# Expert products of the further jobs: plain float32 operands in place of split pairs, and the next rows turned ahead of the down product

## Chip, core and metric

One core of a Trainium2 chip runs the kernel in one launch. The metric is the device time of that launch in microseconds (us), the median of several runs.

## What is computed

One block of a decoder: a convolution branch and an attention branch are merged by gates and added to the input, and a mixture of experts follows. Only the experts matter here. Each of the 2048 tokens picks 2 of 64 experts; its normalized row of 1024 numbers goes through each of the two.

```
def expert_block(args):
    xb, e = args
    hb = jax.nn.silu(xb @ w_gate[e]) * (xb @ w_up[e])
    return hb @ w_down[e]
```

w_gate[e] and w_up[e] are 1024 x 256, w_down[e] is 256 x 1024, all float32. The two results of a token are weighted and added to its row afterwards.

## The kernel before

The kernel runs six stages one after another: project, attend, merge, route, experts, combine. The route stage writes a table that lists for each expert the rows that chose it. The experts stage works in **jobs** of up to 128 rows of one expert. Jobs 0 to 63 are the first tiles of the 64 experts ("first jobs"). Where an expert has more than 128 rows, a further tile follows: the "further jobs", number 64 and up. Their count and their experts are known only at run time, so each engine reads the count from job_sb and runs them in a loop with conditions (over_further_jobs).

One job takes these steps. The buffers are double, and b is the job's parity:
- SyncE (SP) loads gate and up weights (weights_gate_up, 2 x 1 MB, L1903) and down weights (weights_down, 1 MB, L1907) with load_gate_up and load_down.
- VectorE (DVE) writes the list of row numbers (index, L2278). POOL gathers the rows by it from memory into rows (gather, L2090, an indirect DMA).
- TensorE (PE) turns the rows in 8 transposes into x_bank (turn_rows, L2145).
- ScalarE (ACT) takes xT_hi from x_bank (high_x, L2216), DVE the rest xT_lo (lower_x, L2289). Both are float32r. In the same way gate and up weights are split in two halves of 2048 columns each: ACT makes gu_hi (high_gate_up, L2210), DVE makes gu_lo (lower_gate_up, L2284).
- PE makes gate and up products in gu_bank (gate_up, by pair_matmuls, L91 to L93): for each of 8 chunks hi x hi, hi x lo and lo x hi, 24 products of 512 columns.
- ACT applies silu (gate, L2222), DVE multiplies by up (times_up, L2295), PE turns the result (turn_hidden, L2165, two transposes), ACT takes it as hT (take_hidden, L2227).
- PE makes the down product on plain float32 operands (down, L2175). A plain float32 product appears in the trace as two records, so the 4 products of a job are 8 records.
- ACT takes y out of PSUM (take_y, L2233). POOL scatters it to memory (scatter, L2098, an indirect DMA).

The order of the work on each engine is written out by hand. For the further jobs it is the list `parts` given to over_further_jobs: in each turn the parts run in that order, those marked True for job n+1 (ahead), those marked False for job n. For job 63, the last first job, the same parts run once in front of the loop, with n = 63 and 64. In one turn the engines do this, in order:
- PE: gate_up(n), turn_hidden(n), turn_rows(n+1), down(n)
- ACT: high_gate_up(n+1), gate(n), take_hidden(n), high_x(n+1), take_y(n)
- DVE: index(n+1), lower_gate_up(n+1), times_up(n), lower_x(n+1), take_list(n)
- POOL: gather(n+1), scattered(n-1), scatter(n)
- SP: load_gate_up(n+1), which waits until the buffer's former weights are split (gu_lo_ready), and load_down(n+1), which waits for the down product of job n-1 (down_done)

Of the kernel before, what the change touches and what calls it, by code (L numbers as in the profile page):

```python
# [30 lines left out]
P = 128  # L31
# [52 lines left out]
def raw(ap):  # L84

    return ap.bitcast(F32)
# [1824 lines left out]
def stage_experts(nc, weights, hn_d, table_d, jobs_d, y_d):  # L1911
# [10 lines left out]
    with ExitStack() as ctx:  # L1922
# [13 lines left out]
        rows = sb("rows", [P, 2, D])  # L1936
        xT_hi = sb("xT_hi", [P, 2, DC, P], F32R)
        xT_lo = sb("xT_lo", [P, 2, DC, P], F32R)
        silu = sb("silu", [P, DE])
        hidden = sb("hidden", [P, 2, DE])  # L1940
        hT = sb("hT", [P, 2, HC, P])
# [84 lines left out]
        @block.sync  # L2026
        def _(sp):
            sp.dma_start(table[:, :], table_rows[0:P, :]).then_inc(table_loaded, 16)
            sp.dma_start(job_sb[:, 0:1 + 2 * MORE_JOBS], jobs_d).then_inc(jobs_loaded, 16)

            def load_gate_up(n, b, e):
                wait(sp, gu_lo_ready, n * 2 + 2)
                weights.load_gate_up(sp, b, e)

            def load_down(n, b, e):
                wait(sp, down_done, n + 1)
                weights.load_down(sp, b, e)

            load_gate_up(2, 0, 2)
            load_gate_up(3, 1, 3)  # L2040
            wait(sp, jobs_loaded, 16)
            count = sp.value_load(job_sb[0:1, 0:1], min_val=0, max_val=MORE_JOBS)

            def load_list(j):
                e = sp.value_load(job_sb[0:1, bass.ds(j + 1, 1)], min_val=0, max_val=EXPERTS - 1)
                first = sp.value_load(job_sb[0:1, bass.ds(j + (1 + MORE_JOBS), 1)], min_val=0, max_val=SEQ - P)
                sp.dma_start(columns[:, bass.ds(j, 1)], table_rows[bass.ds(first, P), bass.ds(e, 1)],
                             allow_slow_non_contiguous=True).then_inc(columns_loaded, 16)

            with sp.Fori(0, MORE_JOBS // LISTS) as i:  # L2050
                with sp.If(i * LISTS < count):
                    for k in range(LISTS):
                        with sp.If(i * LISTS + k < count):
                            load_list(i * LISTS + k)

                    sp.sem_inc(pair_passed["SP"], 1)
            load_down(2, 0, 2)
            with sp.Fori(2, EXPERTS // 2) as q:
                for b in range(2):
                    n = q * 2 + b  # L2060
                    load_gate_up(n, b, n)
                    load_down(n - 1, 1 - b, n - 1)
            load_down(EXPERTS - 1, 1, EXPERTS - 1)

            def further(n, b, q):
                j = n - EXPERTS + 1
                e = sp.value_load(job_sb[0:1, j:j + 1] if isinstance(j, int) else job_sb[0:1, bass.ds(j, 1)],
                                  min_val=0, max_val=EXPERTS - 1)
                load_gate_up(n, b, e)
                load_down(n, b, e)  # L2070

            over_further_jobs(sp, [(True, further)])

# [59 lines left out]
        def _(pe):  # L2133
# [15 lines left out]
            def gate_up(n, b, half):  # L2149
# [7 lines left out]
                if half:  # L2157
                    m.then_inc(gu_done, 1)

            def turn_hidden(n, b):  # L2160

                pe.wait_ge(hidden_ready, n + 2)
                by_chunk = hidden[:, b, :].rearrange("t (p c) -> t c p", c=HC)
                for c in range(HC):
                    m = nc.tensor.transpose(gu_bank[:, b, c * P:(c + 1) * P], by_chunk[:, c, :], ident[:, :])  # L2165
                m.then_inc(hidden_turned, 1)
# [25 lines left out]
            down(EXPERTS - 2, 0, EXPERTS // 2 - 1)  # L2192

            def further_products(n, b, q):
                gate_up(n, b, 0)
                gate_up(n, b, 1)
                turn_hidden(n, b)

            over_further_jobs(pe, [(False, further_products), (True, turn_rows), (False, down)])

        @block.scalar
        def _(act):
# [53 lines left out]
            take_hidden(EXPERTS - 2, 0)  # L2256
            take_y(EXPERTS - 2, 0)

            def further_weights(n, b, q):
                for half in range(2):  # L2260
                    high_gate_up(n, b, q, half)

            def further_hidden(n, b, q):
                gate(n, b)
                take_hidden(n, b)

            over_further_jobs(act, [(True, further_weights), (False, further_hidden),
                                    (True, lambda n, b, q: high_x(n, b)), (False, lambda n, b, q: take_y(n, b))])

        @block.vector  # L2270
        def _(dve):
# [15 lines left out]
            def lower_x(n, b):  # L2287
                wait(dve, x_hi_ready, n + 1)
                nc.vector.tensor_tensor(xT_lo[:, b, :, :], x_bank[:, :, :].rearrange("p k (c t) -> p (k c) t", t=P),  # L2289
                                        raw(xT_hi[:, b, :, :]), ALU.subtract).then_inc(x_lo_ready, 1)  # L2290

            def times_up(n, b):
                wait(dve, silu_ready, n + 1)
# [35 lines left out]
                j = n - EXPERTS  # L2329
                return columns[:, j:j + 1] if isinstance(j, int) else columns[:, bass.ds(j, 1)]  # L2330

            def further_weights(n, b, q):
                index(n, b, further_list(n))
                for half in range(2):
                    lower_gate_up(n, b, half)

            def further_rows(n, b, q):
                take_list(n, b, list_of(n) if isinstance(n, int) and n < EXPERTS else further_list(n))

            over_further_jobs(dve, [(True, further_weights), (False, lambda n, b, q: times_up(n, b)),  # L2340
                                    (True, lambda n, b, q: lower_x(n, b)), (False, further_rows)])


def stage_combine(nc, h_d, y_d, weight_d, out):
# [130 lines left out]
```

## Time and profile before

| | |
|---|---|
| median of 3 runs | 3007.86 us (3005.77 to 3012.45) |
| profiled execution, its own time | 3009.71 us |
| its span | 3007.8 us |
| mean granted TensorE clock | 0.933 |
| busy share: PE, DVE, ACT, POOL | 85%, 58%, 38%, 17% |
| mean memory traffic | 170 GB/s |

The profile is of one execution. The busy share of an engine is a mean over six stages that have different limits, so it tells what an engine does in total, and not what bounds a stage; for that one reads windows and timelines of the stage itself.

### The profile page before, as it was taken

To read this page: it belongs to the slowest core of one execution; us is meant where nothing else is said; L and a number is where in the kernel's file an instruction comes from. 1 tells how busy PE (TensorE), PEld (TensorE's weight loads), DVE (VectorE), ACT (ScalarE), POOL (GpSimd) and SP (SyncE) were. 2 spreads that over 40 slices of the span, in tenths; PEclk is the share of its full clock that TensorE was granted. 3 is DMA by queue.
4 is the path that set the end of the run, shared out by engine and by line. 5 is a ranking of instruction groups with operands and counts; after the bars stand their busy time and mean duration, and the time that the engine had idled before them with its cause. 6 is when DMAs were issued, how large, how long until landed. Compare 5 with 4: busy or idle time off the path is not lost. (4 is left out here: it accounts for less than half of the span.)

```text
span 3007.8 us, 40627 instructions
## 1 busy us (share of the span) xinstructions
PE 2543.5 (85%) x12335; PEld 2047.1 (68%) x12335; DVE 1730.5 (58%) x2408; ACT 1145.1 (38%) x1622; POOL 509.1 (17%) x465
## 2 busy tenths in 40 slices
PE   4999999999997598899939886997499999999750
PEld 3888889899985487788817665775366666666530
DVE  6576584967712487787845453444455555555425
ACT  4110111134412376677732222212355555656420
POOL 2122222211100011111103221011211111211110
PEclk9999999999998799999969997998699999999975
DMA  5121211213321533434058867554388889988739
GB/s 127 51 84 37 81 49 63 70 71 106 106 95 59 143 86 87 112 100 132 15 141 193 194 171 228 175 174 181 110 334 331 338 341 368 349 335 344 281 133 394
DMA packets 227934, 510.61 MB, mean 170 GB/s; under 512 B 30268, under 2 KB 150076, under 8 KB 189404
## 3 DMA queue, kind: packets, MB, share of 16 engines
q1 hardware_dynamic: 194738, 411.80, 41.5%
q10 hardware_dynamic: 10626, 55.14, 4.5%
q0 software_dynamic: 22448, 42.16, 4.2%
q8 instruction: 63, 1.03, 0.1%
q14 instruction: 59, 0.48, 0.1%
HBM read 413.28 MB, written 133.46 MB: 182 GB/s over the span
## 5 line engine op out<-in xcount | busy, mean ns | idle before, releaser
L91 PE MATMUL project_bank<-project_xnT_hi,project_w_hi 128*128 128x512 f32 (+4 forms) x1352 | 512.1, 379 | 0.8 <-DVE project_xnT_lo L593 0.7
L92 PE MATMUL project_bank<-project_xnT_lo,project_w_hi 128*128 128x512 f32 (+4 forms) x1352 | 499.9, 370 | 0.0
L93 PE MATMUL project_bank<-project_xnT_hi,project_w_lo 128*128 128x512 f32 (+4 forms) x1352 | 497.8, 368 | 0.0
L2284 DVE TENSOR_TENSOR experts_gu_lo<-weights_gate_up,experts_gu_hi 128x2048 fp32r<-128x2048 f32 x136 | 306.4, 2289 | 134.3 <-ACT experts_gu_hi L2210 133.8
L641 DVE SCALAR_TENSOR_TENSOR project_work<-project_work,project_taps 128x2048 f32<-128x2048 f32 x128 | 341.4, 2667 | 18.6 <-DVE project_work L637 0.6
L2210 ACT ACTIVATE experts_gu_hi<-weights_gate_up 128x2048 fp32r<-128x2048 f32 x136 | 259.2, 1911 | 96.5 <-DMA weights_gate_up<-in_w_up_dram 70.6
L91 PEld LDWEIGHTS project_bank<-project_xnT_hi,project_w_hi 128*128 128x128 f32 (+1 forms) x1352 | 252.5, 187 | 35.6 <-issue 6.7
L92 PEld LDWEIGHTS project_bank<-project_xnT_lo,project_w_hi 128*128 128x128 f32 (+1 forms) x1352 | 252.4, 187 | 32.9 <-issue 6.1
L93 PEld LDWEIGHTS project_bank<-project_xnT_hi,project_w_lo 128*128 128x128 f32 (+1 forms) x1352 | 252.6, 187 | 26.9
L1013 DVE TENSOR_TENSOR attend_pT<-attend_t_bank,attend_pT 128x512 fp32r<-128x512 f32 (+3 forms) x352 | 212.5, 615 | 86.2 <-ACT attend_pT L963 83.8
L2175 PE MATMUL experts_y_bank<-weights_down,experts_hT 128*128 128x512 f32 x544 | 248.8, 600 | 3.9 <-issue 3.3
L909 PE MATMUL attend_o_bank<-attend_pT,attend_values 128*128 128x256 f32 x1216 | 226.9, 303 | 13.1 <-DVE attend_pT L1013 12.4
L963 ACT ACTIVATE attend_pT<-attend_t_bank 128x512 fp32r<-128x512 f32 (+3 forms) x352 | 183.8, 540 | 137.0 <-PE attend_t_bank L895 111.0
L91 PE MATMUL experts_gu_bank<-experts_gu_hi,experts_xT_hi 128*128 128x512 f32 x544 | 228.1, 419 | 0.0
L93 PE MATMUL experts_gu_bank<-experts_gu_hi,experts_xT_lo 128*128 128x512 f32 x544 | 215.6, 396 | 0.0
L92 PE MATMUL experts_gu_bank<-experts_gu_lo,experts_xT_hi 128*128 128x512 f32 x544 | 213.5, 392 | 0.0
L2289 DVE TENSOR_TENSOR experts_xT_lo<-experts_x_bank,experts_xT_hi 128x1024 fp32r<-128x1024 f32 x68 | 83.3, 1225 | 208.3 <-ACT experts_xT_hi L2216 186.1
L475 ACT ACTIVATE project_work<-project_bank,project_bias 128x512 f32<-128x512 f32 x64 | 44.2, 690 | 402.2 <-PE project_bank L93 402.2
L882 PE MATMUL attend_s_bank<-attend_keys,attend_q_hi 128*128 128x400 f32 (+5 forms) x352 | 136.0, 386 | 71.1 <-DMA attend_decay<-decay_d 42.5
L895 PE MATMUL attend_t_bank<-attend_ident,attend_probs 128*128 128x128 f32 x1216 | 192.4, 277 | 0.0
L909 PEld LDWEIGHTS attend_o_bank<-attend_pT,attend_values 128*128 128x128 f32 x1216 | 169.1, 190 | 29.0 <-issue 14.3
L2175 PEld LDWEIGHTS experts_y_bank<-weights_down,experts_hT 128*128 128x128 f32 x544 | 103.5, 193 | 111.0 <-issue 105.8
(249 smaller groups left out, 4316.8 us busy)
## 6 DMA issues: line engine op xcount, KB each, us to landing
weights_gate_up<-in_w_gate_dram SPq DMA_DIRECT2D x68, 1024.0 KB
weights_gate_up<-in_w_up_dram SPq DMA_DIRECT2D x68, 1024.0 KB
weights_down<-in_w_down_dram SPq DMA_DIRECT2D x68, 1024.0 KB, 6.6
project_w_raw<-in_w_in_dram SPq DMA_DIRECT2D x36, 512.0 KB, 4.1
qk_d<-project_work SPq DMA_DIRECT2D x16, 1032.0 KB, 5.3
gate_d<-project_work ACTq DMA_DIRECT2D x16, 1024.0 KB, 3.9
merge_gates<-gate_d SPq DMA_DIRECT2D x64, 256.0 KB, 5.3
merged_d<-merge_m_pair SPq DMA_DIRECT2D x64, 256.0 KB, 4.1
```

Source lines behind the costliest of these rows:

```text
L91: pe.matmul(out, lhs[0], rhs[0], start=first, stop=False)
L92: pe.matmul(out, lhs[0], rhs[1], start=False, stop=False)
L93: return pe.matmul(out, lhs[1], rhs[0], start=False, stop=last)
L641: nc.vector.scalar_tensor_tensor(out=work[:, 2, 0:SEQ], in0=work[:, 1, META - 1 + q:META - 1 + q + SEQ], scalar=taps[:, bass.ds(ct, 1), q] ...
L882: nc.tensor.matmul(out, q_hi[:, h, qs], keys[:, h, a - PAD:e - PAD], start=True, stop=False)
L895: m = nc.tensor.transpose(t_bank[:, j % 3, (t % 4) * P:(t % 4 + 1) * P], probs[:, u % BUF, t * P:(t + 1) * P], ident[:, :])
L909: m = nc.tensor.matmul(out, values[:, h, t, :], pT[:, j % 3, t % 4].rearrange("p k q -> p (k q)"), start=t == 0, stop=t == last)
L963: nc.scalar.activation(pT[:, j % 3, 0:n, 0, :], t_bank[:, j % 3, 0:n * P].rearrange("p (t q) -> p t q", q=P), ACT.Copy)\
L1013: nc.vector.tensor_tensor(pT[:, j % 3, 0:n, 1, :], t_bank[:, j % 3, 0:n * P].rearrange("p (t q) -> p t q", q=P), raw(pT[:, j % 3, 0:n, 0, ...
L2175: m = nc.tensor.matmul(y_bank[:, b, half, :], hT[:, b, c, :], down_raw[:, b, c, cols], start=c == 0, stop=c == HC - 1)
L2210: nc.scalar.activation(gu_hi[:, b, :, cut, :], gu_raw[:, b, :, cut, :], ACT.Copy)\
L2284: nc.vector.tensor_tensor(gu_lo[:, b, :, cut, :], gu_raw[:, b, :, cut, :], raw(gu_hi[:, b, :, cut, :]), ALU.subtract).then_inc(gu_lo_ready, 1)
```

## The change

For further jobs from 64 on, the loop jobs, gate and up products use plain float32 operands: xT, a copy of the turned rows, and the loaded weights themselves. The split of rows and weights is gone for them, and with it 24 products of float32r pairs; 8 plain products take their place. Job 63, which runs in front of the loop, keeps the split. The order of the parts changes on PE, ACT and DVE. The load of gate and up weights for a further job now waits for gu_done, the products that read the buffer before, since no split frees it any more.

```diff
+        xT = sb("xT", [P, 2, DC, P])
...
+            def load_further(n, b, e):
+                wait(sp, gu_done, n + 1)
+                weights.load_gate_up(sp, b, e)
+                load_down(n, b, e)
...
-                load_gate_up(n, b, e)
-                load_down(n, b, e)
+                load_further(n, b, e)
...
+            def gate_up_plain(n, b, q):
+                pe.wait_ge(gu_loaded[b], q * 32 + 32)
+                pe.wait_ge(x_lo_ready, n + 2)
+                for c in range(DC):
+                    m = nc.tensor.matmul(gu_bank[:, b, :], xT[:, b, c, :], gu_raw[:, b, :, c, :],
+                                         start=c == 0, stop=c == DC - 1)
+                m.then_inc(gu_done, 1)
...
             def further_products(n, b, q):
-                gate_up(n, b, 0)
-                gate_up(n, b, 1)
+                if isinstance(n, int):
+                    gate_up(n, b, 0)
+                    gate_up(n, b, 1)
+                else:
+                    gate_up_plain(n, b, q)
+
+            def further_down(n, b, q):
                 turn_hidden(n, b)
-
-            over_further_jobs(pe, [(False, further_products), (True, turn_rows), (False, down)])
+                down(n, b, q)
+
+            over_further_jobs(pe, [(False, further_products), (True, turn_rows), (False, further_down)])
...
-            def further_weights(n, b, q):
-                for half in range(2):
-                    high_gate_up(n, b, q, half)
-
-            def further_hidden(n, b, q):
+            def further_products(n, b, q):
                 gate(n, b)
                 take_hidden(n, b)
-
-            over_further_jobs(act, [(True, further_weights), (False, further_hidden),
-                                    (True, lambda n, b, q: high_x(n, b)), (False, lambda n, b, q: take_y(n, b))])
+                take_y(n, b)
+
+            over_further_jobs(act, [(False, further_products)])
...
+            def take_x(n, b):
+                wait(dve, x_turned, n + 3)
+                wait(dve, gu_done, n + 1)
+                nc.vector.tensor_copy(xT[:, b, :, :], x_bank[:, :, :].rearrange("p k (c t) -> p (k c) t", t=P))\
+                  .then_inc(x_lo_ready, 1)
...
-            def further_weights(n, b, q):
+            def further_index(n, b, q):
                 index(n, b, further_list(n))
-                for half in range(2):
-                    lower_gate_up(n, b, half)
...
-            over_further_jobs(dve, [(True, further_weights), (False, lambda n, b, q: times_up(n, b)),
-                                    (True, lambda n, b, q: lower_x(n, b)), (False, further_rows)])
+            over_further_jobs(dve, [(True, further_index), (True, lambda n, b, q: take_x(n, b)),
+                                    (False, lambda n, b, q: times_up(n, b)), (False, further_rows)])
```

PE, the end of a turn of the loop before: the last products of job n, then turn_hidden (L2165), turn_rows of job n+1 (L2145) and down (L2175).

```order
L93 MATMUL experts_gu_bank<-experts_gu_hi,experts_xT_lo 128x512
L2165 MATMUL experts_gu_bank<-experts_ident_e,experts_hidden 128x128 x2
L2019 UNCONDITIONAL_BRANCH
L2016 REGISTER_ALU
L2016 COMPARE_AND_BRANCH
L2141 ISA
L2142 REGISTER_ALU
L2145 MATMUL experts_x_bank<-experts_ident_e,experts_rows 128x128 x8
L2016 UNCONDITIONAL_BRANCH
L2019 COMPARE_AND_BRANCH
```

What the change makes of it: PE, the turn in the changed loop, where L2169 is gate_up_plain, L2150 turn_rows, L2178 turn_hidden and L2188 down:

```order
L2169 MATMUL experts_gu_bank<-weights_gate_up,experts_xT 128x512 x8
L2020 UNCONDITIONAL_BRANCH
L2017 REGISTER_ALU
L2017 COMPARE_AND_BRANCH
L2146 ISA
L2147 REGISTER_ALU
L2150 MATMUL experts_x_bank<-experts_ident_e,experts_rows 128x128 x8
L2017 UNCONDITIONAL_BRANCH
L2020 COMPARE_AND_BRANCH
L2175 REGISTER_ALU
L2178 MATMUL experts_gu_bank<-experts_ident_e,experts_hidden 128x128 x2
L2182 ISA
```

Before, turn_hidden stands between the products and turn_rows. In the change it has moved from ahead of turn_rows to behind it, directly in front of down.

DVE, the same turn before, from the split of the second half of job n+1's weights (L2284) over times_up (L2295) to lower_x (L2289):

```order
L2284 TENSOR_TENSOR experts_gu_lo<-weights_gate_up,experts_gu_hi 128x2x1024 [waits experts_gu_hi_ready]
L2016 UNCONDITIONAL_BRANCH
L2019 COMPARE_AND_BRANCH
L74 REGISTER_ALU
L2295 TENSOR_TENSOR experts_hidden<-experts_silu,experts_gu_bank 128x256 [waits experts_silu_ready,experts_hidden_turned]
L2019 UNCONDITIONAL_BRANCH
L2016 COMPARE_AND_BRANCH
L74 REGISTER_ALU
L2289 TENSOR_TENSOR experts_xT_lo<-experts_x_bank,experts_xT_hi 128x1024 [waits experts_x_hi_ready]
```

DVE, the turn in the changed loop, where L2310 is take_x and L2316 times_up:

```order
L2293 TENSOR_SCALAR experts_from_row<-experts_columns 128x1
L2017 UNCONDITIONAL_BRANCH
L2017 COMPARE_AND_BRANCH
L74 REGISTER_ALU
L74 REGISTER_ALU [waits experts_x_turned]
L2310 COPY experts_xT<-experts_x_bank 128x1024 [waits experts_gu_done]
L2017 UNCONDITIONAL_BRANCH
L2020 COMPARE_AND_BRANCH
L74 REGISTER_ALU
L2316 TENSOR_TENSOR experts_hidden<-experts_silu,experts_gu_bank 128x256 [waits experts_silu_ready,experts_hidden_turned]
```

The work on the turned rows of job n+1 stood behind times_up of job n and now stands ahead of it.

## Rows read from the trace of the kernel before

**Rows 1.** The page's busy times, and its group of the down products.

```profile
PE 2543.5 (85%) x12335; PEld 2047.1 (68%) x12335; DVE 1730.5 (58%) x2408; ACT 1145.1 (38%) x1622; POOL 509.1 (17%) x465
...
L2175 PE MATMUL experts_y_bank<-weights_down,experts_hT 128*128 128x512 f32 x544 | 248.8, 600 | 3.9 <-issue 3.3
```

**Rows 2.** Timeline of PE: start us, us, instruction, [idle before <- releaser].

```profile
2763.72 3.60 PE L2175 MATMUL experts_y_bank<-weights_down,experts_hT 128*128 128x512 f32 x8
2767.16 1.05 PE L2145 MATMUL experts_x_bank<-experts_ident_e,experts_rows 128*128 128x128 f32 x8
...
2840.39 1.97 PE L2145 MATMUL experts_x_bank<-experts_ident_e,experts_rows 128*128 128x128 f32 x8 [2.21 <-DMA experts_rows<-hn_d,experts_from_row]
...
2859.99 1.97 PE L2145 MATMUL experts_x_bank<-experts_ident_e,experts_rows 128*128 128x128 f32 x8 [5.02 <-DMA experts_rows<-hn_d,experts_from_row]
2861.76 4.80 PE L2175 MATMUL experts_y_bank<-weights_down,experts_hT 128*128 128x512 f32 x8
...
2874.68 0.70 PE L2165 MATMUL experts_gu_bank<-experts_ident_e,experts_hidden 128*128 128x128 f32 x2 [2.65 <-DVE experts_hidden L2295]
2880.19 1.97 PE L2145 MATMUL experts_x_bank<-experts_ident_e,experts_rows 128*128 128x128 f32 x8 [4.81 <-DMA experts_rows<-hn_d,experts_from_row]
...
2895.88 1.97 PE L2145 MATMUL experts_x_bank<-experts_ident_e,experts_rows 128*128 128x128 f32 x8
2897.64 3.93 PE L2175 MATMUL experts_y_bank<-weights_down,experts_hT 128*128 128x512 f32 x8
2901.01 0.79 PE L91 MATMUL experts_gu_bank<-experts_gu_hi,experts_xT_hi 128*128 128x512 f32 x1
...
2906.66 0.39 PE L93 MATMUL experts_gu_bank<-experts_gu_hi,experts_xT_lo 128*128 128x512 f32 x1
2908.44 0.51 PE L2165 MATMUL experts_gu_bank<-experts_ident_e,experts_hidden 128*128 128x128 f32 x2 [1.38 <-DVE experts_hidden L2295]
2909.58 3.70 PE L2175 MATMUL experts_y_bank<-weights_down,experts_hT 128*128 128x512 f32 x8 [0.64 <-ACT experts_hT L2227]
```

**Rows 3.** Windows: length, busy us of PE, PEld, DVE, ACT, POOL; PEclk, DMA share, GB/s.

```profile
2600.00:2800.00 200.00, 194.76 (x800) 134.84 (x799) 117.51 (x114) 120.16 (x115) 38.51 (x38) 1.00 0.88 337
...
2860.00:2865.00 5.00, 5.00 (x13) 3.14 (x14) 1.38 (x3) 1.02 (x1) 0.00 (x0) 0.58 0.02 5
...
2870.00:2875.00 5.00, 2.35 (x11) 1.64 (x10) 4.62 (x3) 1.84 (x2) 2.98 (x1) 0.94 1.00 348
```

**Rows 4.** Timeline of POOL: gathers (L2090) and scatters (L2098).

```profile
2798.87 1.02 POOL L2090 DMA_INDIRECT experts_rows<-hn_d,experts_from_row  x1 [7.72 <-DVE experts_to_row L2300]
...
2831.48 1.05 POOL L2090 DMA_INDIRECT experts_rows<-hn_d,experts_from_row  x1 [3.69 <-issue]
...
2868.73 0.99 POOL L2098 DMA_INDIRECT y_d<-experts_y_sb,experts_to_row  x1 [15.94 <-ACT experts_y_sb L2233]
2870.03 2.98 POOL L2090 DMA_INDIRECT experts_rows<-hn_d,experts_from_row  x1 [0.31 <-issue]
...
2890.55 2.95 POOL L2090 DMA_INDIRECT experts_rows<-hn_d,experts_from_row  x1 [0.48 <-issue]
2903.75 0.99 POOL L2098 DMA_INDIRECT y_d<-experts_y_sb,experts_to_row  x1 [10.25 <-ACT experts_y_sb L2233]
```

**Rows 5.** Timeline of ACT.

```profile
2866.82 1.03 ACT L2233 ACTIVATE experts_y_sb<-experts_y_bank 128x1024 f32<-128x1024 f32 x1 [3.57 <-PE experts_y_bank L2175]
```

**Rows 6.** Timeline of SP's queue: the issues of gate weights for jobs 65 and 67.

```profile
2827.02 0.34 SPq L1903 DMA_DIRECT2D weights_gate_up<-in_w_gate_dram  x1
...
2868.83 0.34 SPq L1903 DMA_DIRECT2D weights_gate_up<-in_w_gate_dram  x1
```

**Rows 7.** Timeline of DVE.

```profile
2863.39 1.23 DVE L2289 TENSOR_TENSOR experts_xT_lo<-experts_x_bank,experts_xT_hi 128x1024 fp32r<-128x1024 f32 x1 [8.98 <-ACT experts_xT_hi L2216]
...
2869.80 4.49 DVE L2284 TENSOR_TENSOR experts_gu_lo<-weights_gate_up,experts_gu_hi 128x2048 fp32r<-128x2048 f32 x2 [5.02 <-ACT experts_gu_hi L2210]
...
2894.71 0.41 DVE L2295 TENSOR_TENSOR experts_hidden<-experts_silu,experts_gu_bank 128x256 f32<-128x256 f32 x1
```

## Prediction

> **What bounds the kernel now.** I began with the page's busy table and slices, to see how much of the kernel the change can reach. TensorE is busy 85% of the span [rows 1], but the change leaves the 64 first jobs alone but for what follows job 63's product; only the further jobs see it. Their number is read from the matmul groups: L2175 has 544 records, eight per job (3.60 us for eight [rows 2]), so 68 jobs, 4 of them further: 64 to 67. I call R64 to R67 the starts of their row transposes on TensorE (L2145): 2840.39, 2859.99, 2880.19 and 2895.88 [rows 2]. Everything to be won or lost lies between 2827.02, where the load for job 65 is issued [rows 6], and the start of the combine stage.
>
> Next the windows. Among the first jobs TensorE is busy 194.76 of 200 us at a granted clock of 1.00; behind R65 the clock is 0.58, in part the low level of 1.2 GHz [rows 3]. So the further jobs are not bound by TensorE. The timeline names the bound: the transposes of jobs 64, 65 and 66 wait for DMA experts_rows [rows 2]. I then followed that gather back on POOL. The rows of job 66 are gathered at 2870.03, right behind the scatter of job 64 at 2868.73 [rows 4], which waits for y of job 64 at 2866.82 [rows 5], which waits for the down product at 2861.76 [rows 2], which TensorE issues behind the transposes of job 65. So the circle is: transposes, down product of the job before, y, scatter, gather, next transposes. It takes 19.60, 20.20 and 15.69 us, 55.5 in all. Gate and up products (6.04 us, 2901.01 to 2907.05) and the splitting lie in its shadow, except in job 67, which nothing follows.
>
> Two parts of the circle are longer than they must be. First, the gathers of jobs 65 to 67 keep POOL busy for 2.9 to 3.0 us each, that of job 64 for 1.05, the first jobs' for 1.02 [rows 4]. The long ones begin inside a splitting operation of VectorE: for job 66 its two halves run 4.49 us from 2869.80 [rows 7]. The gather ends 0.97 us after the first half (2869.80 + 2.24 = 2872.04, to 2873.01), as if it had started only there. I read that as POOL being held out by the subtraction of two SBUF tensors. Second, from the end of POOL's work to the transposes pass 7.9, 7.2 and 7.2 us, but only 2.4 for job 67, the one gather that has no gate and up load beside it: the one for job 67 is issued at 2868.83 [rows 6], and the DMA engines move 348 GB/s at share 1.00 in 2870 to 2875 [rows 3].
>
> **The change, part by part.**
> Job 64 starts: SyncE now waits for job 63's product (about 2830.4 instead of 2827.02) before it loads job 65's gate and up [rows 6]. POOL still issues job 64's gather at 2831.48, so gather and load overlap as before, yet the load (2 MB at 348 GB/s: 6 us) is over near 2838, where the rows have come in only near 2840 till now. R64 between 2836.4 and 2840.4; I take -1.5.
> Splitting: for four jobs ACT's copies and DVE's subtractions of the weights go (4 x 4.49 = 18 us of busy time on DVE), worth nothing by themselves, since they lay behind the waiting gather; with them goes the hold on POOL: 1.9 us per gather, three times. For job 64's gather there is no such gain.
> New order: the down product stood 1.77 us behind R. Now VectorE first copies the turned rows (take_x), and only behind that, in its own queue, does times_up follow; then turn_hidden, hT, down. No row shows this copy; the nearest is the subtraction from the same bank, 1.23 us, and on the other side ACT's copy of as many elements from PSUM, 1.03 [rows 5, 7]; I take 1.2, since it is the same engine. times_up is 0.41 [rows 7], and turn_hidden to down 1.14 us at the high clock (2908.44 to 2909.58), 0.2 more at the low one. With transposes of 1.05 to 1.16 or 1.97 us [rows 2] the down product starts at R+4.0 (2.4 GHz) or R+5.1 (1.2 GHz): 2.2 to 3.3 us later than now. That is the change's cost in the circle.
> From down to gather: 8.27 us now (2861.76 to 2870.03), 7.4 if it runs at the high clock (2897.64 to the scatter at 2903.75, plus the 1.3 from scatter to gather) [rows 2, 4]. For the first turn, behind a long idle time, I take 8.7.
> Landing: the loads of 66 and 67 now wait for the products of 64 and 65, which end near R65 and R66, so they are through well before the next gather and still some 8 us ahead of their own use. Landing 2.4 us; for job 65, whose tile may hold more rows, 3.0. Ends: 2.4 and 7.2.
> Product: 16 plain records at the pace of L2175 (3.60 us for eight) make 7.2 us against 6.04. In the circle TensorE then needs 4.0 + 3.4 (down, 2897.64 to 2901.01) + 7.2 = 14.6 us at the high clock, just inside the gather's path, so this stays hidden but takes all the slack there was.
> Sum. R64 to R65, behind 8 us of idle TensorE, clock low: 5.1 + 8.7 + 1.05 + 3.0 = 17.8 against 19.60: -1.8. R65 to R66: 4.0 + 7.4 + 1.05 + 2.4 = 14.9 at the high clock, 5.1 + 8.4 + 1.05 + 2.4 = 17.0 at the low; TensorE's idle time ahead of R now is below 1 us, so I take 15.5, nearer the high: -4.7. R66 to R67 the same 15.5 against 15.69: -0.2. Tail, to the end of job 67's product: now 11.2 us (2895.88 to 2907.05), then 14.6 to 16.6, I take 15.2: +4.0. What follows (silu, down, scatter, barrier, combine) is as before. In all -1.5 - 1.8 - 4.7 - 0.2 + 4.0 = **-4.2 us**.
> The sum is made against the profiled execution: span 3007.8, time 3009.71, so 1.9 us around it. The median of the runs, 3007.86, is 1.9 lower; taken off there, 3003.7 us. A measurement of this kernel tells 0.2%, 6.0 us, from no change; the three runs before span 6.7.
>
> Beside the hold on POOL stands the Trainium skill, SBUF — State Buffer, "Who interferes with whom": a VectorE instruction with two SBUF inputs contends with a GpSimd instruction that reads SBUF, and whoever started first holds the port for the whole instruction. Job 66's gather agrees. But the same section infers that building descriptors needs the write side only, so that tensor_tensor would not stall such a DMA; by that the 2.9 us are something else and stay (rival B), and the sum would be +1.3. That the gather ends one gather's time behind the subtraction's half speaks against it.
>
> **The rivals.**
> A, more is won, 18%: the clock stays high in all four turns and job 64's rows land by 2836.4. Then -4.0, -2.6, -5.3, -0.8 and +3.4: -9.3, 2998.6 us. For it: a gap of 1.38 us left turn_hidden at its fast 0.51 (2908.44). Against: one of 2.65 us did not (0.70 at 2874.68) [rows 2].
> B, the gathers stay at 2.95 us, 12%: because their waits are counted in registers, say. Against: the first jobs' gathers in the loop do that too and take 1.02. +1.9, +1.8, +1.8: 3009.2.
> C, landing stays at 7.2 us for jobs 65 and 66, 10%: the scatter ahead of the gather, not the loads, is what it waits for. +4.2 and +4.8: 3012.7. Against: job 67's has a scatter ahead of it too.
> D, slower, 15%: the clock. The new order cuts TensorE's work at R into transposes, a gap of 1.7 us, two transposes, a gap of 0.6, the down product; today transposes and down are one piece, and the clock rises inside down (4.80 us at 2861.76 instead of 3.60). If it stays at 1.2 GHz through down, eight records at twice 0.43 us make 6.8, 3.2 more than now at the high clock. Each turn is then 5.1 + (7.4 + 3.2) + 1.05 + 2.4 = 19.2, the first 19.8, the tail 5.1 + 6.6 + 7.2 = 18.9: +0.2, -1.0, +3.5, +7.7, with R64 +8.9; if it rises only inside the products, some 1.5 us more each, +15. Middle +12: 3019.9. The turning point is where the clock rises: it costs more than the forecast gains once down takes above some 5.4 us in all four turns. For it: the 0.58 behind R65 [rows 3]. Against: gate and up now run right up to the transposes.
> The Trainium skill, TensorE: Matmul & The Clock Gate, "HAM oscillation", warns of this: work cut up by waits falls back to half rate and must warm up again each time. The windows agree for today's turns; whether gaps this short do it no row tells.
>
> **How the numbers follow.** The forecast has 45%, its own range 3000 to 3007. Predicted 3003.7. Leaving out a fourth of A and most of D gives 2998 to 3014. Faster by over 6.0 us: most of A and a tenth: 0.25. Slower by over 6.0: D and a little of C: 0.17. Within: 0.58.
>
> **What would show it.** Gathers of 65 to 67 at 1.0 us on POOL. R64 near 2839; R to R about 17.8, 15.5, 15.5. down at R+4 to 5. Gate and up products of 7.2 us, 16 records. Loads of 66 and 67 issued at the products' ends; DMA idle when the gather goes. The prediction is wrong if a transpose waits over 4 us for its rows behind a 1 us gather (C), if down takes over 5.4 us (D), or if the next product waits for its weights.

## The result, and the profile after

The change made the kernel slower by a little: the ratio to the kernel before is 1.0023, 95% interval 1.0015 to 1.0031 (medians 3013.55 and 3004.97 us). Two of the 20 runs of the change took 3142 and 9305 us, in a slow state of the chip, and are left out of the ratio. I had forecast 4.2 us less, and called slower by over 0.2% the least likely outcome. Single executions of either kernel differ by some 10 us, so traces are compared here over one stretch that holds all that the change touches: from the start of job 62's down product to the first load of the combine stage. Before it runs from 2821.22 to 2921.05, 99.8 us; after from 2819.97 to 2925.53, 105.6 us: +5.7.

Timeline of PE after, the stretch without job 63's split products and some rows of the later turns (start us, us, instruction, [idle before <- releaser]). L2150 are the row transposes, L2178 turn_hidden, L2188 down, L2169 the plain products.

```profile
2819.97 3.67 PE L2188 MATMUL experts_y_bank<-weights_down,experts_hT 128*128 128x512 f32 x8 [1.21 <-issue]
...
2839.70 1.97 PE L2150 MATMUL experts_x_bank<-experts_ident_e,experts_rows 128*128 128x128 f32 x8 [10.61 <-DMA experts_rows<-hn_d,experts_from_row]
2843.32 0.70 PE L2178 MATMUL experts_gu_bank<-experts_ident_e,experts_hidden 128*128 128x128 f32 x2 [1.65 <-DVE experts_hidden L2316]
2844.54 5.37 PE L2188 MATMUL experts_y_bank<-weights_down,experts_hT 128*128 128x512 f32 x8 [0.52 <-issue]
2849.74 7.03 PE L2169 MATMUL experts_gu_bank<-weights_gate_up,experts_xT 128*128 128x512 f32 x16
2858.51 1.15 PE L2150 MATMUL experts_x_bank<-experts_ident_e,experts_rows 128*128 128x128 f32 x8 [1.74 <-DMA experts_rows<-hn_d,experts_from_row]
2861.62 0.70 PE L2178 MATMUL experts_gu_bank<-experts_ident_e,experts_hidden 128*128 128x128 f32 x2 [1.95 <-DVE experts_hidden L2316]
2862.96 6.41 PE L2188 MATMUL experts_y_bank<-weights_down,experts_hT 128*128 128x512 f32 x8 [0.64 <-ACT experts_hT L2246]
...
2877.05 1.15 PE L2150 MATMUL experts_x_bank<-experts_ident_e,experts_rows 128*128 128x128 f32 x8 [0.82 <-DMA experts_rows<-hn_d,experts_from_row]
...
2881.59 5.40 PE L2188 MATMUL experts_y_bank<-weights_down,experts_hT 128*128 128x512 f32 x8 [0.94 <-ACT experts_hT L2246]
...
2894.65 1.15 PE L2150 MATMUL experts_x_bank<-experts_ident_e,experts_rows 128*128 128x128 f32 x8 [0.80 <-DMA experts_rows<-hn_d,experts_from_row]
...
2898.89 5.40 PE L2188 MATMUL experts_y_bank<-weights_down,experts_hT 128*128 128x512 f32 x8 [0.64 <-ACT experts_hT L2246]
2904.12 7.03 PE L2169 MATMUL experts_gu_bank<-weights_gate_up,experts_xT 128*128 128x512 f32 x16
```

Against [rows 2]: from job 65 on the transposes wait only 0.8 to 1.7 us for their rows, where those of jobs 65 and 66 waited 5.0 and 4.8. In return a gap of 1.65 to 1.95 us stands behind the transposes, released by times_up (DVE L2316), where before down followed at once (before, the wait for times_up stood ahead of the transposes, 2.65 us in the turn of R66 [rows 2]), and down begins 4.2 to 4.8 us behind them instead of 1.8. And down itself takes 5.37 to 6.41 us, where it took 4.80 in the turn of R65 and 3.93 in that of R67.

Windows of the same kernel (length, busy us of PE, PEld, DVE, ACT, POOL; PEclk, DMA share, GB/s):

```profile
2844.00:2849.00 5.00, 4.48 (x8) 2.01 (x8) 0.00 (x0) 0.38 (x1) 0.00 (x0) 0.60 0.00 0
...
2863.00:2868.00 5.00, 5.00 (x6) 2.14 (x7) 0.00 (x0) 0.00 (x0) 0.00 (x0) 0.50 0.14 57
```

TensorE is fully busy in the second window and runs at 0.50, the level of 1.2 GHz, throughout. Timelines of POOL, of DVE and of ACT after:

```profile
2853.30 1.03 POOL L2095 DMA_INDIRECT experts_rows<-hn_d,experts_from_row  x1 [0.45 <-issue]
...
2872.77 1.04 POOL L2095 DMA_INDIRECT experts_rows<-hn_d,experts_from_row  x1 [0.31 <-issue]
...
2890.58 1.03 POOL L2095 DMA_INDIRECT experts_rows<-hn_d,experts_from_row  x1 [0.49 <-issue]
```

```profile
2860.01 1.23 DVE L2310 COPY experts_xT<-experts_x_bank 128x1024 f32<-128x1024 f32 x1 [16.62 <-PE experts_x_bank L2150]
2861.15 0.41 DVE L2316 TENSOR_TENSOR experts_hidden<-experts_silu,experts_gu_bank 128x256 f32<-128x256 f32 x1
```

```profile
2857.05 0.38 ACT L2241 ACTIVATE experts_silu<-experts_gu_bank 128x256 f32<-128x256 f32 x1 [6.08 <-PE experts_gu_bank L2169]
```

The gathers took 1.03 to 1.04 us instead of 2.9 to 3.0 [rows 4], and the copy, which no row before showed, 1.23. Term by term, in us:

| term | forecast | measured | from |
|---|---|---|---|
| down of job 62 to R64 | -1.5 | +0.6 | 19.17 to 19.73 |
| R64 to R65 | -1.8 | -0.8 | 19.60 to 18.81 |
| R65 to R66 | -4.7 | -1.7 | 20.20 to 18.54 |
| R66 to R67 | -0.2 | +1.9 | 15.69 to 17.60 |
| R67 to the product's end | +4.0 | +5.3 | 11.17 to 16.50 |
| to the combine stage | 0 | +0.4 | 14.00 to 14.38 |
| sum | -4.2 | +5.7 | |

### The profile page after: what moved, and what is told of

It reads as the page before. It is cut to its first block and busy times, and to the rows that moved or that the text cites. A ratio compares the mean times of both kernels' runs of the same rounds, so it can differ in the third digit from the quotient of the medians.

```text
span 3012.3 us, 40485 instructions
## 1 busy us (share of the span) xinstructions
PE 2546.0 (85%) x12303; PEld 2038.0 (68%) x12303; DVE 1712.2 (57%) x2400; ACT 1126.3 (37%) x1610; POOL 503.4 (17%) x465
## 3 DMA queue, kind: packets, MB, share of 16 engines
q8 instruction: 63, 1.03, 0.1%
## 5 line engine op out<-in xcount | busy, mean ns | idle before, releaser
L2299 DVE TENSOR_TENSOR experts_gu_lo<-weights_gate_up,experts_gu_hi 128x2048 fp32r<-128x2048 f32 x128 | 288.3, 2289 | 99.8 <-ACT experts_gu_hi L2229 99.5
L2229 ACT ACTIVATE experts_gu_hi<-weights_gate_up 128x2048 fp32r<-128x2048 f32 x128 | 244.5, 1912 | 80.4 <-DMA weights_gate_up<-in_w_up_dram 55.2
L2188 PE MATMUL experts_y_bank<-weights_down,experts_hT 128*128 128x512 f32 x544 | 253.2, 609 | 7.6 <-issue 4.4
L91 PE MATMUL experts_gu_bank<-experts_gu_hi,experts_xT_hi 128*128 128x512 f32 x512 | 214.1, 418 | 0.0
L93 PE MATMUL experts_gu_bank<-experts_gu_hi,experts_xT_lo 128*128 128x512 f32 x512 | 203.0, 397 | 0.0
L92 PE MATMUL experts_gu_bank<-experts_gu_lo,experts_xT_hi 128*128 128x512 f32 x512 | 200.8, 392 | 0.0
L2188 PEld LDWEIGHTS experts_y_bank<-weights_down,experts_hT 128*128 128x128 f32 x544 | 104.8, 194 | 118.4 <-issue 110.1
```

Of the source, the lines that this page charges most:

```text
L91: pe.matmul(out, lhs[0], rhs[0], start=first, stop=False)
L92: pe.matmul(out, lhs[0], rhs[1], start=False, stop=False)
L93: return pe.matmul(out, lhs[1], rhs[0], start=False, stop=last)
L2188: m = nc.tensor.matmul(y_bank[:, b, half, :], hT[:, b, c, :], down_raw[:, b, c, cols], start=c == 0, stop=c == HC - 1)
L2229: nc.scalar.activation(gu_hi[:, b, :, cut, :], gu_raw[:, b, :, cut, :], ACT.Copy)\
L2299: nc.vector.tensor_tensor(gu_lo[:, b, :, cut, :], gu_raw[:, b, :, cut, :], raw(gu_hi[:, b, :, cut, :]), ALU.subtract).then_inc(gu_lo_ready, 1)
```

## The experiments

Ratios are to the kernel before, run beside each on the same chip. "Stretch" is the one above: 99.8 us before, 105.6 after. "Landing" is the time from the end of POOL's gather to the transposes.

**1. The old order with plain operands.** Theory 1 says that the order costs, its rival that the plain products do.

```diff
             def further_products(n, b, q):
...
                     gate_up_plain(n, b, q)
-            def further_down(n, b, q):
                 turn_hidden(n, b)
-                down(n, b, q)
-            over_further_jobs(pe, [(False, further_products), (True, turn_rows), (False, further_down)])
+            over_further_jobs(pe, [(False, further_products), (True, turn_rows), (False, down)])
...
-            over_further_jobs(dve, [(True, further_index), (True, lambda n, b, q: take_x(n, b)),
-                                    (False, lambda n, b, q: times_up(n, b)), (False, further_rows)])
+            over_further_jobs(dve, [(True, further_index), (False, lambda n, b, q: times_up(n, b)),
+                                    (True, lambda n, b, q: take_x(n, b)), (False, further_rows)])
```

> Plain operands and the late load as in the change, but the order of the kernel before on PE (product, turn_hidden, turn_rows, down) and DVE (times_up ahead of take_x). Theory 1, the new order is what costs: down again stands 1.8 us behind R, the gather's path is 1.8 + 8.4 + 1.0 + 3.1 = 14.3 us, and TensorE itself becomes the bound: down to R+6.2, product 7.0, 2.8 to turn_hidden, 0.5: turns of 16.4 us (now 18.8, 18.5, 17.6), the product of job 67 ends at R67+12.2 (now 16.5). Against the kernel before: -5 to -6 us, 0.998. Rival, the plain product is what costs: turns stay at 17.6 to 18.8 and the time at 1.002.

Measured: 0.9953 (0.9937 to 0.9969), stretch 89.7 us. Timeline of PE:

```profile
2849.70 0.50 PE L2178 MATMUL experts_gu_bank<-experts_ident_e,experts_hidden 128*128 128x128 f32 x2 [1.40 <-DVE experts_hidden L2313]
2850.13 1.15 PE L2150 MATMUL experts_x_bank<-experts_ident_e,experts_rows 128*128 128x128 f32 x8
2851.12 3.60 PE L2188 MATMUL experts_y_bank<-weights_down,experts_hT 128*128 128x512 f32 x8
2854.55 7.03 PE L2169 MATMUL experts_gu_bank<-weights_gate_up,experts_xT 128*128 128x512 f32 x16
2862.96 0.51 PE L2178 MATMUL experts_gu_bank<-experts_ident_e,experts_hidden 128*128 128x128 f32 x2 [1.38 <-DVE experts_hidden L2313]
2863.38 1.15 PE L2150 MATMUL experts_x_bank<-experts_ident_e,experts_rows 128*128 128x128 f32 x8
```

The sign was as theory 1 had it, and the size larger than the 5 to 6 us that I expected: 14 us by the ratio, 10 by the stretch, with turns of 15.8, 13.3 and 13.5 us, not 16.4. From job 65 on the circle through the gather is gone, the transposes wait for nothing, and one gap of 1.4 us a turn is all that TensorE idles. There the clock stays at 1.00 and down takes 3.60 to 3.70 us. In the turn of R64, behind 9.2 us in which TensorE waits for the rows, down takes 5.32 us in this order too. The plain operands, with the later load that comes with them, are the gain, and the new order more than spends it.

**2. One line of it.** PE keeps the new order; only VectorE's order is the old one (the second hunk above alone).

> The change, with one thing undone: on DVE times_up stands ahead of take_x again. PE keeps the new order. Theory 1 (the wait of times_up behind take_x is the cost, by itself and by the gap it makes for TensorE's clock): turn_hidden follows the transposes at once, down starts at R+2.3 to 3.3 instead of 4.2 to 4.8 and runs at the high clock (3.7 to 4.5 us, now 5.4 to 6.4); turns 14.5 to 16, job 67's product ends at R67+13, 8 to 9 us below the kernel before, 0.997. Rival, TensorE's order by itself costs: down stays at 5.4 us and the time within 2 us of the change.

Measured: 0.9962 (0.9948 to 0.9976), stretch 91.1 us.

```profile
2859.23 1.15 PE L2150 MATMUL experts_x_bank<-experts_ident_e,experts_rows 128*128 128x128 f32 x8 [0.71 <-DMA experts_rows<-hn_d,experts_from_row]
2860.22 0.40 PE L2178 MATMUL experts_gu_bank<-experts_ident_e,experts_hidden 128*128 128x128 f32 x2
2861.57 3.70 PE L2188 MATMUL experts_y_bank<-weights_down,experts_hT 128*128 128x512 f32 x8 [0.94 <-ACT experts_hT L2246]
```

turn_hidden now follows the transposes without a gap, since times_up was done before them. So nearly the whole loss hangs on take_x standing ahead of times_up on VectorE. The 14.5 us between the two stretches (105.6 and 91.1) come almost wholly from two sources: over the four turns down starts 8.8 us sooner (at R+2.9, 2.0, 2.3 and 2.0 instead of 4.8, 4.5, 4.5 and 4.2), and it runs 5.6 us shorter (5.90, 3.70, 3.70, 3.70 instead of 5.37, 6.41, 5.40, 5.40).

**3. The gaps filled.** Is that second part the clock?

```diff
+            def fill(b, count):
+                for c in range(count):
+                    nc.tensor.matmul(gu_bank[:, b, 0:P], ident[:, :], ident[:, :], start=True, stop=True)
+
+            def further_turn(n, b, q):
+                turn_rows(n, b, q)
+                fill(b, 12)
...
                 turn_hidden(n, b)
+                fill(1 - b, 4)
                 down(n, b, q)
...
-            over_further_jobs(pe, [(False, further_products), (True, turn_rows), (False, further_down)])
+            over_further_jobs(pe, [(False, further_products), (True, further_turn), (False, further_down)])
```

> The change, with TensorE's gaps filled: 12 products of the identity (128 columns) behind the transposes and 4 behind turn_hidden, written to the bank that the next product overwrites. They compute nothing that is used. Theory 2, the clock: down falls from 5.4 to 6.4 us to 3.7 in the turns of jobs 65 to 67, turns become 16.5 and 16, the product of job 67 ends at R67+14.8: 5 to 6 us below the change, about 1.000 of the kernel before. If the low clock in down has another cause (the transposes, the weight loads), down stays at 5.4, and the fill only delays turn_hidden: at or above the change, 1.002 to 1.003.

Measured: 1.0001 (0.9987 to 1.0015), stretch 101.1 us, 4.5 below the change.

```profile
2854.99 1.15 PE L2150 MATMUL experts_x_bank<-experts_ident_e,experts_rows 128*128 128x128 f32 x8 [1.75 <-DMA experts_rows<-hn_d,experts_from_row]
2855.99 2.84 PE L2216 MATMUL experts_gu_bank<-experts_ident_e 128*128 128x128 f32 x24
2858.66 0.40 PE L2178 MATMUL experts_gu_bank<-experts_ident_e,experts_hidden 128*128 128x128 f32 x2
2858.90 1.06 PE L2216 MATMUL experts_gu_bank<-experts_ident_e 128*128 128x128 f32 x8
2859.79 3.61 PE L2188 MATMUL experts_y_bank<-weights_down,experts_hT 128*128 128x512 f32 x8
```

```profile
2860.00:2865.00 5.00, 5.00 (x13) 2.13 (x12) 0.00 (x0) 1.02 (x1) 0.00 (x0) 1.00 0.26 64
```

Nothing but useless products was added, and down fell to 3.60 to 3.70 us in all four turns, at a clock of 1.00. Over the four turns down is 8.1 us shorter than in the change, which is what the clock was worth; the fill itself delays its start by 3.8 us, and the stretch is 4.5 us shorter. Turns of 19.5, 16.3 and 16.3 us.

**4. The order alone, on split operands.** The kernel before, with turn_rows ahead of turn_hidden, and high_x and lower_x ahead of take_hidden and times_up. The edit on VectorE, one of three:

```diff
-            over_further_jobs(dve, [(True, further_weights), (False, lambda n, b, q: times_up(n, b)),
-                                    (True, lambda n, b, q: lower_x(n, b)), (False, further_rows)])
+            over_further_jobs(dve, [(True, further_weights), (True, lambda n, b, q: lower_x(n, b)),
+                                    (False, lambda n, b, q: times_up(n, b)), (False, further_rows)])
```

> The kernel before with the new order alone: products stay split, loads wait for the split as before; turn_rows stands ahead of turn_hidden, and high_x and lower_x ahead of times_up and take_hidden. Theory 1: without the gain of the plain operands (the hold on POOL, 1.9 us, and the landing beside a load, 4 us) the order costs its full 3.5 us per turn: turns of 23 us, the product of job 67 ends at R67+15.5, together some 12 to 14 us above the kernel before, 1.004. Rival, the order costs little: turns near 20 us and a time within 0.1% of the kernel before.

Measured: 1.009 (1.0075 to 1.0105), stretch 125.2 us, 25.4 above the kernel before: about twice the 12 to 14 that I had expected.

```profile
2886.70 1.97 PE L2145 MATMUL experts_x_bank<-experts_ident_e,experts_rows 128*128 128x128 f32 x8 [7.74 <-DMA experts_rows<-hn_d,experts_from_row]
2891.71 0.70 PE L2165 MATMUL experts_gu_bank<-experts_ident_e,experts_hidden 128*128 128x128 f32 x2 [3.04 <-DVE experts_hidden L2298]
2893.11 5.42 PE L2175 MATMUL experts_y_bank<-weights_down,experts_hT 128*128 128x512 f32 x8 [0.70 <-ACT experts_hT L2230]
```

Two steps, ACT's high_x and VectorE's lower_x, stand in the gap here; it is 3.04 us, and down starts at R+6.4 and takes 5.42 us (6.57 in the turn of R65). Turns of 25.6, 26.2 and 20.7 us.

**5. The late load alone.** The kernel before, with `wait(sp, gu_done, n + 1)` in place of the wait for the split.

> The kernel before with one piece of the change: the gate and up load of a further job waits for the products (gu_done) and no longer for the split. Order and split stay. Theory 3, landing beside a load costs: job 66's load moves from 2848.2 only to 2852, job 67's from 2868.8 to 2872, both still beside the gather, since the split holds the gather back to 2852.8 and 2873.0. So the gain is small: landing 5 to 7 us, turns 18 to 20 us, 0 to 4 us below the kernel before, 0.999 to 1.000, and the gathers stay at 2.9 us. Rival, the late load by itself is the gain of the plain operands: turns of 16 us, 0.996.

Measured: 1.0004 (0.999 to 1.0018). Timelines of POOL and of SP's queue:

```profile
2852.04 2.88 POOL L2091 DMA_INDIRECT experts_rows<-hn_d,experts_from_row  x1 [0.45 <-issue]
```

```profile
2854.38 0.34 SPq L1903 DMA_DIRECT2D weights_gate_up<-in_w_gate_dram  x1
```

As expected, the split still holds the gather until 2854.92, beside the later load; landing stayed at 7.5 us. By itself this piece gains nothing: 1 lies within the interval, and the stretch is 103.1 us, 3.3 above the kernel before. R64 comes 19.73 us behind job 62's down, 0.56 later than before and just as in the change, which points to the late load for that part of the change's loss.

**6. The hold on POOL put back.** Experiment 1 with two subtractions on VectorE, both inputs in SBUF, once y is ready.

```diff
+            def hold(n, b):
+                wait(dve, y_ready, n + 3)
+                for half in range(2):
+                    cut = slice(KH * half, KH * (half + 1))
+                    nc.vector.tensor_tensor(gu_lo[:, 1 - b, :, cut, :], raw(gu_hi[:, 1 - b, :, cut, :]),
+                                            raw(gu_hi[:, 1 - b, :, cut, :]), ALU.subtract)
```

> e1_plain_old_order with two subtractions of VectorE added behind each turn, both inputs in SBUF, 2.29 us each, started when y is ready; their result is not used. Theory 4, such a subtraction holds POOL's indirect DMAs out: the scatter of each turn, which starts 0.9 us behind y, lasts 2.3 instead of 0.99 us or starts later, the gather behind it moves by 1.3 to 2.3 us, turns by 0.5 to 1.5 us each (there is some slack), together 2 to 4 us above e1, 0.9965. Rival, tensor_tensor does not hold them out: scatters 0.99, gathers 1.03, time as e1, 0.995.

Measured: 1.0033 (1.002 to 1.0047), some 24 us above experiment 1 where I expected 2 to 4. VectorE and POOL:

```profile
2842.03 4.49 DVE L2354 TENSOR_TENSOR experts_gu_lo<-experts_gu_hi 128x2048 fp32r<-128x2048 f32 x2 [3.91 <-ACT experts_y_sb L2249]
2846.44 0.15 DVE L2290 TENSOR_SCALAR experts_from_row<-experts_columns 128x1 int32 x1
```

```profile
2842.88 2.31 POOL L2103 DMA_INDIRECT y_d<-experts_y_sb,experts_to_row  x1 [16.31 <-ACT experts_y_sb L2249]
2847.60 1.03 POOL L2095 DMA_INDIRECT experts_rows<-hn_d,experts_from_row  x1 [2.41 <-DMA y_d<-experts_y_sb,experts_to_row]
```

The hold is there: the five scatters of this loop take 2.31 to 2.42 us instead of 0.99, and the first ends 0.9 us behind the first subtraction. The time is no price for it, though, for I had queued more behind the subtractions than I saw: the index of the next gather stands behind them on VectorE (2846.44), and the gather begins 1.15 us behind it in this turn and in the next. (The profile puts that wait down to the scatter's DMA.) The later gather then goes beside the next load and lands in 7.8 us.

**7. The load beside the gather put back.** Experiment 1 with 2 MB more, into a buffer that nobody reads, behind each down load.

```diff
+                wait(sp, more_loaded, (n - EXPERTS) * 32 + 16)
+                for k in range(2):
+                    sp.dma_start(more[:, k, :, :], weights.sources[k][e].rearrange("(p c) n -> p c n", c=DC))\
+                      .then_inc(more_loaded, 16)
```

> e1_plain_old_order with the load beside the gather put back: behind each down load of a further job SyncE loads another 2 MB of weights into a buffer that nobody reads. Theory 3: from the end of POOL's gather to the transposes pass 7 us in every turn instead of 3 to 4.3; turns of e1 (15.8, 13.3, 13.5) become 18.5, 16.5, 16.5, together 9 us above e1, 0.998 to 0.999. Rival, the loads have nothing to do with the landing: turns and time as e1, 0.995.

Measured: 1.0029 (1.0015 to 1.0044), 23 us above experiment 1 where I expected 9. Timelines of POOL and PE:

```profile
2860.97 1.03 POOL L2103 DMA_INDIRECT experts_rows<-hn_d,experts_from_row  x1 [0.46 <-issue]
```

```profile
2871.83 1.97 PE L2158 MATMUL experts_x_bank<-experts_ident_e,experts_rows 128*128 128x128 f32 x8 [5.49 <-DMA experts_rows<-hn_d,experts_from_row]
```

Landing became 9.8, 10.4 and 7.7 us for jobs 65 to 67, against about 4.2 in experiment 1, where the rows did not make TensorE wait at all. A load beside a gather does cost, and more of it costs more: the first two also met the next job's own load.

**8 and 9. Keeping the last such load away.** In the change and in experiment 1 job 65's load still goes beside job 64's gather. One wait more for SyncE takes it away, added to experiment 1 (8) and to the change (9).

```diff
                 wait(sp, gu_done, n + 1)
+                wait(sp, x_turned, n + 2)
                 weights.load_gate_up(sp, b, e)
```

> e1_plain_old_order, with one wait more: the gate and up load of a further job waits until the rows of the job before are turned (x_turned). It takes away the one load that still goes beside a gather, that of job 65 beside job 64's gather. Theory 3 (a gather beside a load lands late): from the end of job 64's gather to its transposes pass 3 to 4 us instead of 7.7, R64 comes 4 us earlier, and the load is still through before its use. 3 to 5 us below e1, 0.994 of the kernel before. Rival: the landing of job 64's gather hangs on the scatter of job 62 ahead of it, not on the load: no change against e1, 0.9953.

> The change, with the same further wait. Theory 3: R64 4 us earlier, the rest as in the change (turns of 18.8, 18.5, 17.6), 3 to 5 us below the change, 1.001 of the kernel before. It then shows how much of the lost prediction is job 64's landing, which was put at -1.5 us, and that the rest is the order. Rival: as the change, 1.0023.

Measured: 0.9941 (0.9918 to 0.9964) for 8, stretch 86.5 us; 0.9999 (0.9985 to 1.0013) for 9, stretch 101.2 us, 4.4 below the change. Experiment 8, POOL and PE:

```profile
2834.04 1.05 POOL L2096 DMA_INDIRECT experts_rows<-hn_d,experts_from_row  x1 [4.49 <-issue]
```

```profile
2838.80 1.97 PE L2151 MATMUL experts_x_bank<-experts_ident_e,experts_rows 128*128 128x128 f32 x8 [5.23 <-DMA experts_rows<-hn_d,experts_from_row]
...
2869.10 1.15 PE L2151 MATMUL experts_x_bank<-experts_ident_e,experts_rows 128*128 128x128 f32 x8 [1.44 <-DMA experts_rows<-hn_d,experts_from_row]
2870.09 5.30 PE L2189 MATMUL experts_y_bank<-weights_down,experts_hT 128*128 128x512 f32 x8
```

Experiment 9, PE:

```profile
2824.88 1.97 PE L2151 MATMUL experts_x_bank<-experts_ident_e,experts_rows 128*128 128x128 f32 x8 [6.48 <-DMA experts_rows<-hn_d,experts_from_row]
```

In experiment 8 job 64's rows landed in 3.7 us instead of 7.7, and R64 came 3.9 us sooner. Some of it was given back: TensorE now waits 1.4 us for job 66's rows, with that job's own load moved to 2855.7, behind R65. That wait and the 1.38 us ahead of turn_hidden, with 0.51 us of work between them, stand ahead of the transposes and of down, and down took 5.30 us at a clock of 0.50 (2871 to 2873) instead of 3.70. So the clock fell there in the old order as well, with take_x behind times_up. The interval of experiment 8 overlaps that of experiment 1, so only the stretch (3.2 us less) and the landing tell the two apart. It has the lowest ratio of all; it and experiments 1 and 2 beat both kernels.

## Why the prediction was wrong

**What held.** The circle through the gather was the bound of the further jobs: where it was broken (experiment 1), the time fell by 0.47%. The hold on POOL went with the split, 2.9 to 1.03 us, as forecast; experiment 6 put it back on the scatters. So rival B is out. The Trainium skill, SBUF — State Buffer, "Who interferes with whom", infers that tensor_tensor does not stall the building of a DMA's descriptors. The scatters of 2.31 to 2.42 us instead of 0.99 in experiment 6 speak against that inference. What the same section states, that a VectorE instruction with two SBUF inputs contends with a GpSimd instruction that reads SBUF, agrees with them. The plain product took 7.03 us against 7.2 forecast and stayed hidden in the circle. The copy took 1.23 us against 1.2.

**What failed.** First the step "From down to gather", at "7.4 if it runs at the high clock". I took turns of 15.5 us, "nearer the high", because TensorE would idle under 1 us ahead of R. It did idle only 0.8 us ahead of R66 and R67, and the transposes ran fast (1.15 us). But the gaps that the new order makes behind them let the clock fall within the turn: down took 5.40 to 6.41 us in the turns of R65 to R67. Down to gather was 9.81 and 8.99 us for the turns R65 and R66, where 15.5 had left about 7.7 (with the start of down at R+4.3). That is rival D's mechanism, at 15%, and its turning point of 5.4 us in all four turns is what was measured (5.37, 6.41, 5.40, 5.40), though the 5.37 behind R64 is no work of the order, for experiment 1 has 5.32 there; its price, that of down at 1.2 GHz to the end, was nearly reached in one turn only (6.41 of 6.8). Experiment 3 shows that the gaps do it: 8 us over four turns. My row of a single gap of 1.38 us had been a bad guide: in the turn of R65 the engine stood still for 1.74 us ahead of the transposes, 1.95 us behind them and 0.64 us ahead of down, and the granted clock went from 1.00 to 0.81 in 2861 to 2862 and to 0.50 in 2862 to 2863. The Trainium skill, TensorE: Matmul & The Clock Gate, "HAM oscillation", had warned that work cut up by waits falls back to half rate, and these turns agree.

Second, "R64 between 2836.4 and 2840.4; I take -1.5". Measured +0.6. The load, issued at 2829.34, was not away near 2838: in 2838 to 2840 the queue that carries the weights still moved 0.21 MB beside the 0.07 MB of the gather's queue, and the rows came in at 2839.70. Experiment 9 shows that with the load away R64 comes 4.1 us sooner (15.6 us behind job 62's down instead of 19.7). The mechanism was the one I had named for the later turns; here I took the load to be over before the rows.

Third, "Landing 2.4 us; for job 65 3.0". It was 4.2, 3.2 and 3.0 us, 2.7 us more over three turns. I had read the 2.4 of job 67 as the price of a gather without a gate and up load beside it. But the hold itself had helped it: POOL's part ended only at 2893.50, when the scatter and the down load ahead of it were through and the DMA engines stood still. In the change it ends at 2891.61, and the engines are still busy. Windows of the kernel before and of the change:

```profile
2893.00:2894.00 1.00, 0.00 (x0) 0.00 (x0) 1.00 (x1) 0.10 (x1) 0.50 (x1) 1.00 0.00 0
```

```profile
2892.00:2893.00 1.00, 1.00 (x4) 0.52 (x3) 0.00 (x0) 0.00 (x0) 0.00 (x0) 1.00 0.74 258
```

Experiment 6 has the gather of the same job without the hold, at 1.03 us, but late enough to meet idle DMA engines, and it lands in 2.3 us:

```profile
2892.37 1.03 POOL L2095 DMA_INDIRECT experts_rows<-hn_d,experts_from_row  x1 [2.41 <-DMA y_d<-experts_y_sb,experts_to_row]
```

```profile
2895.72 1.75 PE L2150 MATMUL experts_x_bank<-experts_ident_e,experts_rows 128*128 128x128 f32 x8 [1.55 <-DMA experts_rows<-hn_d,experts_from_row]
```

So of the 1.9 us that the hold was to give, 0.7 came back as landing for job 67. For jobs 65 and 66 this was not measured.

Together, against a forecast of -4.2: R64 2.1 us; the three turns 6.2, of which landing 2.7 and down's clock most of the remaining 3.5; the tail 1.3, by down again; and 0.4 behind it. But for rounding that is the way from -4.2 to +5.7, 9.9 us. The start of down behind R was about right (4.84, 4.45, 4.54, 4.24, forecast between 4.0 and 5.1). That the median, 3013.55, still lies between 2998 and 3014 is owed to the room left for rivals; the sign of the forecast was wrong.

Rival A did not come about: the clock did not stay high, and job 64's rows did not land by 2836.4. Rival C, the scatter ahead as the cause of the 7.2 us, falls with experiments 7 to 9: with the scatters unchanged the landing followed the loads.

What stays open: experiments 4, 6 and 7 cost two to eight times what was expected. Lines of their traces suggest why, but no run takes those apart. How much of experiment 1's gain is the hold on POOL and how much the landing was not measured by itself either.

## What to carry to other kernels

When a step is pulled ahead in one engine's queue, ask what stood behind it there and how long the most critical of that had been ready: times_up of job n had been ready for 3 to 13 us (silu of job 64 ends at 2857.43, times_up starts at 2861.15), and queued behind a copy that waits for a gather it cost 14.5 us of the stretch (experiment 2), where the plain operands had won 10.1 (experiment 1). A good half can hide in a bad edit; undo the order and the operands apart before judging either. And price a product on TensorE by what the engine does just ahead of it in the new order, not by its duration in the old.

## What I had not expected of the hardware

An indirect DMA on POOL that begins inside a VectorE subtraction of two SBUF tensors waits it out, and only that one, not a second that stands right behind: a scatter of 0.99 us becomes 2.31 (experiment 6), a gather of 1.03 becomes 2.9 (the kernel before). A gather lands in 2.3 to 2.4 us when the DMA engines stand still (job 67, in the kernel before and in experiment 6), in 3.0 to 4.2 right behind a scatter and a down load (the change), in 7 to 8 beside 2 MB of weights, and in up to 10.4 beside more (experiment 7). TensorE ran a fully busy window of 5 us (2863 to 2868) at 0.50 of its clock right behind gaps of 1.74, 1.95 and 0.64 us, though 7 us of solid work had ended only 6 us earlier (2856.8).
